# z products of a hybrid attention and DeltaNet layer, moved from the attention stage into the delta heads as filler

## Chip, cores and metric

One core of a Trainium2 chip. The metric is the device time of one launch in microseconds, median of three runs.

## The reference

One step of a one-layer encoder with 1024 prompt frames and 8 streams of 16 new frames, model width 1024, all float32:

```
x += 0.5 * SwiGLU_1(norm(x))
proj = norm(x) @ w_in      # q, k, v of 8 attention heads x 64; q, k, v, z of 4 delta heads x 128; beta, decay; 2 gates
yA = softmax attention over the frame's chunk of 64 and 8 chunks before it, with a bias by clipped distance
q, k, v = silu(causal conv of width 4 over proj)        # delta heads; q and k are l2-normalised
ob = gated delta rule (q, k, v, decay, beta), from a triangular solve per block and a scan over the blocks
ob = rmsnorm(ob) * silu(z)
x += (sigmoid(gA) * (yA @ w_branch_a) + sigmoid(gB) * (ob @ w_branch_b)) @ w_mix_out
x += CrossAttn(norm(x), 256 memory tokens)
x += 0.5 * SwiGLU_2(norm(x));  y = final_norm(x)
```

z of a delta head is thus 128 columns of `w_in`; it is first used when the head's output is scaled.

## The kernel before

Feature rows lie on the 128 partitions and all 1152 frames (1024 + 8 x 16) along the free dimension, cut in three thirds of 384. A weight matrix is cut into units of 128 output columns (128 x 1024). SP loads the units into a ring of three buffers (`load_units`, L72); GpSimd (POOL) splits each into an upper and a lower part (`split_units`, L107); TensorE multiplies. A **job** is one unit by one third: 24 products of 128x384 (8 chunks, each as upper by upper, upper by lower, lower by upper). Jobs write PSUM banks 0 and 1 in turn (`g % 2`); ACT evacuates a job's bank, and a job waits until the evacuation of the job that had its bank is counted. `slot` (L55) gives a unit its buffer of the ring.

A **Filler** (L222) cuts jobs into pieces, single products, and hands so many of them to each place of a plan, a list written out by hand: `products` (L238) issues the pieces of one place on TensorE, `finished` (L257) tells ACT which jobs end in a place, so that it evacuates them there.

**Attention** (`attention_phase`, L824): four pairs of heads. A pair has nine jobs of its own (v, q, k, three thirds each; `job` L975, `take` L1102 on ACT), then nine steps of scores, softmax and values (`pair`, L1020, L1128 and L1249), with the pieces of twelve filler jobs between them: the projections q, k, v and z of the delta head of the same number. ACT evacuates the rows of q, k and v into `stash`; DVE applies the convolution (`tap`, L1291) and ACT stores the result to DRAM (`store_row`, L1076). z is stored to DRAM as it is (L1072 to L1074). `turn_v` (L1004) transposes v on TensorE, `copy_v` (L1114) copies it back. The first pair takes its jobs third by third, and v is turned ahead of the last of them, with the first scores within it (`first_jobs`, L985). The three others run in a loop: on ACT, ten loads of bias rows (`load_bias`, L1091), the nine takes, and after the third of them the last conv row's store, the conv tail's store and the loads of the next head's conv state and weights (`next_conv`, L1086, `load_conv`, L1081); after the sixth, v's copies and the loads of the caches (`load_caches`, L1107).

**Delta** (`delta_phase`, L1521): four heads, one after the other, with twelve filler jobs each, the 16 units of the two branch gates; ACT evacuates them to `b_stash` and stores them (`evacuate_these`, L1785). A head on TensorE (`turn`, L1643): filler START; three groups of grams, decay rows and turns (L1656 to L1670), each with filler GROUP behind; filler BEFORE; the turns of Y (L1679); an inversion in 18 rounds over three groups of tiles (L1682 to L1696): a product P by the masked matrix (L1689), filler LEVEL, the turn of Y of two rounds ago (L1634), the correction of the round before (L1626); three W groups (L1703, L1705), with filler W; eight steps of the scan: a product by S (L1713), filler STEP, in steps 4 to 7 a sum of squares for the next head's keys (L1640), and three products (L1720 to L1724), of which DVE makes the next S (L2037); the samples, with two places SAMPLE; products by v8 (L1751); filler END; the three sums of squares for the output's norm (L1760), with filler LAST behind the first two. ACT loads z at round 12 (`load_z`, L1824), takes its silu ahead of step 0 (L1872), and at the head's end stores the states and, at the start of the next head, waits for those stores and loads the next states (L1831 to L1834). The output of head i - 1 is scaled by z in the rounds 6 to 11 of head i (`finish_output`, L1944). The plans count pieces per place (L1366); END takes what is left of 288:

```
PLAN, FIRST_PLAN = (28, 22, 20, 1, 8, 10, 10, 12), (0, 20, 14, 1, 8, 8, 8, 9)
#                   START, GROUP, BEFORE, LEVEL, W, STEP, SAMPLE, LAST
filler = Filler(3, 4, [0, 8, 20, 8, 22, 8, 24, 8] + [23, 8] + [30, 8] + [25, 8] * 3 + [6, 16])
```

Between the places of the attention's plan stand the turns of the probabilities, two per step. The phases and their units per turn are `turn_sizes` (L649); `weight_units` (host) lays out the units, and `nth_unit` (L760) reorders the first three of the attention.

Of the kernel before, what the change touches and what calls it, by code (L numbers as in the profile page):

```python
# [71 lines left out]
def load_units(sp, k, first, turns, turn, at_turn=None, then=None):  # L72
# [3 lines left out]
    def one(i, j):  # L76
        back, last = last_use(j, turn)
        if not (isinstance(i, int) and i < back):
            sp.wait_ge(k.unit_split.sem, k.unit_split.at(turn * i + (last + 1 - turn * back)))
        sp.dma_start(k.w_raw[slot(j, turn)][:, :], k.units[turn * i + (first + k.nth_unit(k.phase, j))])\  # L80
            .then_inc(k.raw_landed[slot(j, turn)].sem, 16)
# [7 lines left out]
    if turns > 1:  # L89
        with sp.Fori(1, turns) as i:  # L90
            if at_turn:
                at_turn(i)
            for j in range(turn):
                one(i, j)
    k.ahead = units_ahead(k)
    for j in range(k.ahead):
        users = sharing(j, turn) or [turn - 1]
        sp.wait_ge(k.unit_split.sem, k.unit_split.at(turn * (turns - 1) + users[-1] + 1))
        sp.dma_start(k.w_raw[j][:, :], k.units[first + turns * turn + k.nth_unit(k.phase + 1, j)]).then_inc(k.raw_landed[j].sem, 16)
# [122 lines left out]
class Filler:  # L222
# [4 lines left out]
    def __init__(self, main, units, plan, ahead=0):  # L227


        self.main, self.units, self.plan, self.ahead = main, units, plan, ahead  # L230
        self.count = 3 * units
# [6 lines left out]
    def products(self, k, pe, i, place, xh, xl):  # L238

        turn, per_turn = self.main + self.units, 3 * (self.main + self.units)  # L240
        first = sum(self.plan[:place])
        for m in range(first, first + self.plan[place]):
            g, r = 3 * self.main + m // self.PIECES, m % self.PIECES
            u, n, part, c = g // 3, g % 3, r // KD, r % KD
            if r == 0:
                if n == 0:
                    pe.wait_ge(k.unit_split.sem, k.unit_split.at(turn * i + (turn * self.ahead + u + 1)))

                pe.wait_ge(k.evacuated.sem, k.evacuated.at(per_turn * i + (per_turn * self.ahead + g + 1)))
            w = (k.w_lo if part == 2 else k.w_hi)[slot(u, turn)]  # L250
# [391 lines left out]
class Core:  # L642


    def __init__(self, nc, ctx):
# [3 lines left out]
        self.turn_sizes, self.phase, self.ahead, self.split_ahead = (2 * KD, 6, 7, 4, KD, KD, 2, KD, 6), 0, 0, False  # L649
# [110 lines left out]
    def nth_unit(self, phase, j):  # L760

        return (2, 0, 1)[j] if phase == 2 and j < 3 else j
# [61 lines left out]
def attention_phase(nc, k, norm, decay, head, xh, xl, x, x_to, work):  # L824
# [31 lines left out]
    filler = Filler(3, 4, [0, 8, 20, 8, 22, 8, 24, 8] + [23, 8] + [30, 8] + [25, 8] * 3 + [6, 16])  # L856

    DONE = 9 + filler.count
# [17 lines left out]
    def sync(sp):  # L876
# [7 lines left out]
        load_units(sp, k, k.next_unit, PAIRS, 7, then=store_x)  # L884

    def gpsimd(pool):
        split_units(pool, k, PAIRS, filler.jobs(), (7, 8) + filler.jobs()[2:], (0, 0, 0))

    def tensor(pe):
# [85 lines left out]
        def job(i, g, u, n, between=None):  # L975
            if n == 0:
                pe.wait_ge(k.unit_split.sem, k.unit_split.at(7 * i + (u + 1)))

            pe.wait_ge(k.evacuated.sem, k.evacuated.at(DONE * i + max(g + 1, 2)))
            tiles = [(k.w_hi[u][:, c * P:(c + 1) * P], k.w_lo[u][:, c * P:(c + 1) * P],  # L980
# [4 lines left out]
        def first_jobs():  # L985
            for n in range(3):
# [6 lines left out]
                for u in range(3):  # L993
                    if (n, u) == (2, 2):
                        turn_v(0)
                        job(0, 8, u, n, lambda: first_scores(0))
                        continue
# [22 lines left out]
        def pair(i):  # L1020
            for s in range(STEPS):
# [7 lines left out]
                filler.products(k, pe, i, 2 * s, xh, xl)  # L1029
# [3 lines left out]
                filler.products(k, pe, i, 2 * s + 1, xh, xl)  # L1033
                turn_probs(i, s, 1)
            filler.products(k, pe, i, 2 * STEPS, xh, xl)
            values(i, STEPS - 1)
            filler.products(k, pe, i, 2 * STEPS + 1, xh, xl)

        first_jobs()
        pair(0)  # L1040
        with pe.Fori(1, PAIRS) as i:
            for g in range(9):
# [3 lines left out]
                if g == 5:  # L1046
# [4 lines left out]
    def scalar(act):  # L1051
        def evacuate(i, g):
# [4 lines left out]
            if n == 0 and u == 1:  # L1057
                act.wait_ge(k.z_stored.sem, k.z_stored.at(16 * i + 16))
            elif n == 0:
                act.wait_ge(k.convolved.sem, k.convolved.at(3 * i + (0, 0, 1, 2)[u] + 1))  # L1060
            if u == 3:
                act.activation(row[:, CW - 1 + n * THIRD:CW - 1 + (n + 1) * THIRD], src[:, 0:THIRD], ACT.Copy)\
                    .then_inc(k.evacuated.sem, 1)
            elif n < 2:
# [7 lines left out]
            if n == 2 and u == 3:  # L1072
# [1839 lines left out]
```

## Time and profile before

| | |
|---|---|
| median of 3 runs | 3450.75 us (3444.57 to 3454.02) |
| profiled execution | 3447.24 us, span of its instructions 3445.5 us |
| TensorE products / weight loads busy | 3254.2 us (94%) / 3093.1 us (90%) |
| DVE / ACT / GpSimd busy | 37% / 20% / 28% |
| granted TensorE clock, mean | 0.983 |
| attention | about 980 to 1470 us: first pair to 1097.3, then 1222.1, 1346.6, 1469.9 |
| delta stage | 1470 to 2000 us: heads end (last sum of squares) at 1612.9, 1744.1, 1875.8, 2000.4 |

How to read it: PE is TensorE, PEld its weight loads, POOL GpSimd; ACTq is ACT's queue at work on an issue of a DMA. The ends of matmuls are modelled, so two rows overlap, and how long work takes is read from start to start. A granted clock of 1.00 is 2.4 GHz, 0.50 is 1.2 GHz. A row `x8` stands for eight instructions that follow each other; a float32 product of 128 columns counts as two.

### The profile page before, as it was taken

What the parts mean: (1) busy time and instruction counts of PE and PEld (TensorE: products, weight loads), DVE (VectorE), ACT (ScalarE), POOL (GpSimd) and SP (SyncE); (2) the same over time, 40 slices, a digit from 0 to 9 for tenths busy, and PEclk for the clock granted to TensorE, in tenths of its full rate; (3) what the DMA queues carried; (4) which work ended last, traced back from release to release, by engine and by line L of the source; (5) the groups of instructions that cost most, each with busy time, mean ns of one, the idle gap of its engine ahead of it and who ended that gap; (6) DMA issues with size and microseconds to landing.
All of it is one profiled execution on the core that took longest, in us unless ns stands there. A gap on an engine that the chain in (4) does not pass through costs nothing. (4 is left out here: it accounts for less than half of the span.)

```text
span 3445.5 us, 50361 instructions
## 1 busy us (share of the span) xinstructions
PE 3254.2 (94%) x19977; PEld 3093.1 (90%) x19977; DVE 1286.4 (37%) x2289; ACT 681.7 (20%) x1318; POOL 947.6 (28%) x436
## 2 busy tenths in 40 slices
PE   6999999999989999989998979999799999999998
PEld 5999999999878889888887879988598999999997
DVE  3232333333435635643442454331225323233324
ACT  5100000000123323344433332133311000000001
POOL 3433333333312223111001023221123333333331
PEclk9999999999999999999999999999899999999999
DMA  5311111111232232212112144024401111111111
GB/s 189 136 37 49 43 43 43 42 37 37 86 115 78 101 127 92 108 48 84 70 48 86 44 158 158 25 99 150 148 31 43 43 47 39 42 43 43 37 49 55
DMA packets 96544, 254.05 MB, mean 74 GB/s; under 512 B 11552, under 2 KB 52640, under 8 KB 93728
## 3 DMA queue, kind: packets, MB, share of 16 engines
q1 hardware_dynamic: 45568, 146.95, 13.0%
q10 hardware_dynamic: 50848, 105.25, 8.5%
q8 instruction: 97, 1.59, 0.2%
q14 instruction: 31, 0.25, 0.0%
HBM read 199.83 MB, written 52.33 MB: 73 GB/s over the span
## 5 line engine op out<-in xcount | busy, mean ns | idle before, releaser
L124 POOL TENSOR_TENSOR w_hi<-w_raw,zero 128x1024 fp32r<-128x1024 f32 x201 | 384.5, 1913 | 2221.2 <-PE psum L157 1324.4
L157 PE MATMUL psum<-x_hi,w_hi 128*128 128x384 f32 x3024 | 597.1, 337 | 44.6 <-DVE x_lo L2254 32.5
L157 PE MATMUL psum<-x_lo,w_hi 128*128 128x384 f32 x3024 | 595.7, 337 | 0.0
L157 PE MATMUL psum<-x_hi,w_lo 128*128 128x384 f32 x3024 | 590.0, 334 | 0.0
L157 PEld LDWEIGHTS psum<-x_hi,w_hi 128*128 128x128 f32 x3024 | 532.5, 189 | 54.5 <-issue 46.6
L157 PEld LDWEIGHTS psum<-x_lo,w_hi 128*128 128x128 f32 x3024 | 534.7, 189 | 2.1 <-issue 0.2
L157 PEld LDWEIGHTS psum<-x_hi,w_lo 128*128 128x128 f32 x3024 | 531.3, 188 | 0.0
L127 POOL TENSOR_TENSOR w_lo<-w_raw,w_hi 128x1024 fp32r<-128x1024 f32 x201 | 494.4, 2460 | 15.8
L407 DVE TENSOR_TENSOR f_hid<-psum,f_gate 128x384 f32<-128x384 f32 x132 | 73.6, 557 | 857.5 <-PE psum L157 857.5
L357 ACT ACTIVATE f_gate<-psum 128x384 f32<-128x384 f32 x132 | 64.8, 493 | 1478.2 <-PE psum L157 1474.5
L157 PE MATMUL psum<-f_h_hi,w_hi 128*128 128x384 f32 x1056 | 269.5, 336 | 0.0
L157 PE MATMUL psum<-f_h_lo,w_hi 128*128 128x384 f32 x1056 | 267.9, 334 | 0.0
L157 PE MATMUL psum<-f_h_hi,w_lo 128*128 128x384 f32 x1056 | 267.9, 334 | 0.0
L251 PE MATMUL psum<-x_hi,w_hi 128*128 128x384 f32 x912 | 203.4, 351 | 0.6 <-POOL w_lo L127 0.5
L251 PE MATMUL psum<-x_lo,w_hi 128*128 128x384 f32 x912 | 199.3, 347 | 0.0
L251 PE MATMUL psum<-x_hi,w_lo 128*128 128x384 f32 x912 | 198.1, 346 | 0.0
L157 PEld LDWEIGHTS psum<-f_h_hi,w_hi 128*128 128x128 f32 x1056 | 190.4, 188 | 3.6 <-issue 1.2
L157 PEld LDWEIGHTS psum<-f_h_lo,w_hi 128*128 128x128 f32 x1056 | 190.7, 188 | 0.0
L157 PEld LDWEIGHTS psum<-f_h_hi,w_lo 128*128 128x128 f32 x1056 | 190.6, 188 | 0.0
L422 DVE SCALAR_TENSOR_TENSOR x_late<-psum,x_late 128x384 f32<-128x384 f32 x264 | 145.1, 556 | 109.9 <-PE psum L157 109.9
L422 DVE SCALAR_TENSOR_TENSOR x_early<-psum,x_early 128x384 f32<-128x384 f32 x264 | 145.0, 556 | 107.2 <-PE psum L157 107.0
L251 PEld LDWEIGHTS psum<-x_hi,w_hi 128*128 128x128 f32 x912 | 159.8, 190 | 6.0 <-issue 2.7
(283 smaller groups left out, 3274.0 us busy)
## 6 DMA issues: line engine op xcount, KB each, us to landing
w_raw<-units SPq DMA_DIRECT2D x224, 512.0 KB, 3.6
gate_dram<-b_stash ACTq DMA_DIRECT2D x48, 192.0 KB, 1.9
e_gate<-gate_dram ACTq DMA_DIRECT2D x48, 192.0 KB, 2.5
a_kc<-k_cache ACTq DMA_DIRECT2D x4, 2048.0 KB, 8.9
a_vc<-v_cache ACTq DMA_DIRECT2D x4, 2048.0 KB, 14.7
x_sk<-mem_k ACTq DMA_DIRECT2D x8, 1024.0 KB, 9.0
proj_dram<-a_cv ACTq DMA_DIRECT2D x12, 576.0 KB, 2.7
b_pad<-proj_dram SPq DMA_DIRECT2D x12, 576.0 KB, 5.3
```

Of the source, the lines that this page charges most:

```text
L124: pool.tensor_tensor(k.w_hi[s][:, :], k.w_raw[s][:, :], k.zero[:, 0:1].to_broadcast([P, D]), ALU.add)\
L127: pool.tensor_tensor(k.w_lo[s][:, :], k.w_raw[s][:, :], k.w_hi[s][:, :].bitcast(F32), ALU.subtract).then_inc(k.unit_split.sem, 1)
L157: mm = pe.matmul(out, wl if part == 2 else wh, (xl if part == 1 else xh)[:, n0:n1], start=(part == 0 and i == 0), stop=(part == 2 and i == ...
L251: mm = pe.matmul(k.ps[g % 2][:, 0:THIRD], w[:, c * P:(c + 1) * P], (xl if part == 1 else xh)[:, c, n * THIRD:(n + 1) * THIRD], start=(r == 0),
L357: act.activation(gate[:, n, :], k.ps[g % NPS][:, 0:THIRD], ACT.Silu).then_inc(k.gate_ready.sem, 1)
L407: dve.tensor_tensor(hid[:, j % 2, :], up, gate[:, n, :], ALU.mult).then_inc(k.hid_made.sem, 1)
L422: dve.scalar_tensor_tensor(out=xs, in0=k.ps[g % NPS][:, 0:THIRD], scalar=0.5, in1=xs, op0=ALU.mult, op1=ALU.add).then_inc(k.x_added.sem, 1)
```

## The change

z of delta head 0 stays filler of the attention, in the last pair; z of heads 1 to 3 becomes the third of five filler units in its own head, and ACT copies it into its tile in SBUF without a way through DRAM. In the attention, v of the next pair takes z's place as filler; pairs 1 to 3 begin with q. The first pair's turn of v and first scores come behind its last job, and its plan has 14 pieces in the first place. On ACT, the last conv row's store and the conv loads come ahead of the first take of pairs 1 to 3; silu(z) moves into step 3. The delta plans get new places: AFTER (behind the turns of Y), a second one per round (behind the correction) and a second one per step (behind its last product). The filler's first job of a turn now waits for two evacuations at once (`max(g + 1, 2)`), as a head of 15 jobs ends in the bank in which the next one starts.

```
-PLAN, FIRST_PLAN = (28, 22, 20, 1, 8, 10, 10, 12), (0, 20, 14, 1, 8, 8, 8, 9)
+PLAN, FIRST_PLAN = (30, 22, 14, 10, (1, 2), 8, 10, 1, 6, 9), (0, 18, 14, 6, (0, 1), 8, 7, 0, 5, 8)
...
+    def head_plan(own, units, start, group, before, after, level, w, step, behind, sample, last):
+        p = own + [start] + [group] * 3 + [before, after] + list(level) * LV + [w] * 3 + [step, behind] * 8 + \
+            [sample] * 2 + [0] + [last] * 2
+        p[-3] = 3 * units * Filler.PIECES - sum(p)
...
+    later_heads = Filler(0, 5, head_plan([], 5, *PLAN), shift=-1)
+    first_head = Filler(0, 4, head_plan([36] + [6] * KEYS, 4, *FIRST_PLAN))
...
+            fill(pe, i, AFTER)
             pe.wait_ge(k.x_started.sem, k.x_started.at(3 * i + 3))
...
-                fill(pe, i, LEVEL + r)
+                fill(pe, i, LEVEL + 2 * r)
                 if 2 <= r < LV - 1:
                     turn_level(pe, i, r - 2)
                 if r >= 1:
                     correct(pe, i, r - 1)
+                fill(pe, i, LEVEL + 2 * r + 1)
...
-                fill(pe, i, STEP + t)
+                fill(pe, i, STEP + 2 * t)
...
                     .then_inc(k.o_done.sem, 1)
+                fill(pe, i, STEP + 2 * t + 1)
...
             for g in products:
-                act.wait_ge(k.dense_done.sem, k.dense_done.at(12 * i + (g + 1)))
+                act.wait_ge(k.dense_done.sem, k.dense_done.at(jobs_to(i) + (g + 1)))
+                if later and g // 3 == ZED:
+                    act.wait_ge(k.o_scaled.sem, k.o_scaled.at(3 * i))
+                    act.activation(z[:, third(g % 3)], k.ps[g % ND][:, 0:THIRD], ACT.Copy).then_inc(k.evacuated.sem, 1)
+                    continue
...
-            act.wait_ge(k.z_landed.sem, k.z_landed.at(16 * i + 16))
-            act.activation(z[:, :], z[:, :], ACT.Silu).then_inc(k.silued.sem, 1)
...
                 if t == 3:
+                    if isinstance(i, int) and i == 0:
+                        act.wait_ge(k.z_landed.sem, k.z_landed.at(16))
+                    else:
+                        act.wait_ge(k.evacuated.sem, k.evacuated.at(15 * i + (6 + ND)))
+                    act.activation(z[:, :], z[:, :], ACT.Silu).then_inc(k.silued.sem, 1)
...
 # Filler.products: the wait of a job
-                pe.wait_ge(k.evacuated.sem, k.evacuated.at(per_turn * i + (per_turn * self.ahead + g + 1)))
+                pe.wait_ge(k.evacuated.sem, k.evacuated.at(per_turn * i + (per_turn * self.ahead + 3 * self.shift + max(g + 1, 2))))
...
 # attention
+    first_pair = Filler(3, 4, period=6, slots=FIRST_SLOTS, plan=[14, 8, 18, 8, 20, 8, 22, 8] + [23, 8] + [30, 8] + [23, 8] * 3 + [6, 14])
+    later_pairs = Filler(3, 4, period=6, slots=LATER_SLOTS, plan=[0, 8, 20, 8, 22, 8, 24, 8] + [23, 8] + [30, 8] + [25, 8] * 3 + [6, 16])
...
         first_jobs()
+        turn_v(0)
+        first_scores(0)
         pair(0)
         with pe.Fori(1, PAIRS) as i:
-            for g in range(9):
+            for g in range(3, 9):
                 if g == 8:
                     first_scores(i)
                 job(i, g, g // 3, g % 3)
-                if g == 5:
+                if g == 3:
                     turn_v(i)
...
+        copy_v(0)
         pair(0)
         with act.Fori(1, PAIRS) as i:
             load_bias(i)
-            for g in range(9):
-                if g == 0:
+            next_conv(i - 1)
+            load_conv(i)
+            for g in range(3, 9):
+                if g == 3:
                     act.wait_ge(k.kv_stored.sem, k.kv_stored.at(32 * i + 32))
...
-                if g == 2:
-                    next_conv(i - 1)
-                    load_conv(i)
-                if g == 5:
+                if g == 3:
                     copy_v(i)
                     load_caches(i)
```

Units: 7 in the first turn of the attention (with v of pair 1), 6 in each of the next three (the sixth is v of the next pair, in the last turn z of head 0), 4 in delta head 0 and 5 in each later one. `host_unit` takes them from the host's unchanged order, and SP's loops run their last turn unrolled. In all, the attention has 75 jobs for 84, the delta heads 57 for 48.

## Rows read from the trace of the kernel before

Columns of the windows: stretch and length in us; busy us and count (x) of PE, PEld, DVE, ACT, POOL; granted clock; DMA share; GB/s. Columns of a timeline: start, us, engine, line, operation, out<-in, count, and in brackets the idle time before it and who ended it.

**Rows 1.** Windows: attention pair 1; 4 us of head 0; delta heads 1, 2, 3.

```profile
1097.30:1222.10 124.80, 122.17 (x872) 110.74 (x872) 62.23 (x113) 39.95 (x95) 30.91 (x15) 1.00 0.29 105
1482.00:1486.00 4.00, 4.00 (x11) 3.09 (x11) 1.15 (x2) 1.62 (x4) 0.00 (x0) 0.50 0.05 17
1612.90:1744.10 131.20, 118.90 (x791) 108.87 (x790) 51.74 (x111) 49.23 (x99) 17.03 (x8) 1.00 0.19 66
1744.10:1875.80 131.70, 118.91 (x791) 108.86 (x791) 51.72 (x111) 49.22 (x99) 17.02 (x8) 1.00 0.18 65
1875.80:2000.40 124.60, 114.53 (x781) 106.87 (x780) 50.31 (x108) 37.06 (x78) 16.96 (x8) 1.00 0.16 55
```

**Rows 2.** Waits of TensorE in the attention: us in total, times, longest.

```profile
PE psum L939 <- DVE a_sc L1288: 10.4, 9, 7.3
PE psum L157 <- ACT a_stash L1062: 2.6, 3, 1.2
```

**Rows 3.** Waits of TensorE in the delta heads, the same columns.

```profile
PE psum L1689 <- DVE b_MT L2000: 6.3, 4, 2.2
...
PE psum L1656 <- DVE b_vb L1980: 5.2, 3, 2.1
```

**Rows 4.** Timeline of PE, start of pair 1: start, duration, instructions.

```profile
1098.83 1.55 PE L157 MATMUL psum<-x_lo,w_hi 128*128 128x384 f32 x8
1100.21 1.55 PE L157 MATMUL psum<-x_hi,w_lo 128*128 128x384 f32 x8
```

**Rows 5.** Timeline of ACT and its queue (ACTq), start of pair 1.

```profile
1096.78 0.49 ACT L1062 ACTIVATE a_stash<-psum 128x384 f32<-128x384 f32 x1 [2.71 <-PE psum L251]
...
1098.45 0.62 ACTq L1100 DMA_DIRECT2D a_bias<-bias_dram  x1
...
1104.46 0.49 ACT L1104 ACTIVATE a_v<-psum 128x384 f32<-128x384 f32 x1 [7.19 <-issue]
...
1110.38 0.40 ACTq L1079 DMA_DIRECT2D proj_dram<-a_cv  x1
...
1112.33 0.36 ACTq L1084 DMA_DIRECT2D a_cw<-conv_w  x1
```

**Rows 6.** Timeline of PE, first pair.

```profile
999.58 0.80 PE L894 MATMUL psum<-a_k,a_q 64*128 64x128 f32 x4 [2.38 <-ACT a_vns L1119]
...
1011.89 0.48 PE L939 MATMUL psum<-ident,a_sc 128*128 128x128 f32 x1 [7.33 <-DVE a_sc L1288]
```

**Rows 7.** Timelines of ACT's queue and of DVE, first pair.

```profile
1001.25 1.86 ACTq L1100 DMA_DIRECT2D a_bias_s<-bias_dram  x4
...
1007.51 0.11 DVE L1258 MEMSET a_bias<- 64x64 f32 x1 [8.86 <-DMA a_bias_s<-bias_dram]
```

**Rows 8.** Timeline of ACT, end of head 1 and start of head 2.

```profile
1745.99 0.48 ACT L1791 ACTIVATE b_stash<-psum 128x384 f32<-128x384 f32 x1
...
1753.54 0.49 ACT L1838 ACTIVATE b_eg<-psum 128x384 f32<-128x384 f32 x1 [0.65 <-ACT b_stash L1791]
```

**Rows 9.** Timeline of PE, one round of the inversion of head 1.

```profile
1656.13 0.94 PE L1689 MATMUL psum<-b_X,b_MT 128*128 128x128 f32 x6
...
1658.16 0.94 PE L1689 MATMUL psum<-b_X,b_MT 128*128 128x128 f32 x6
```

**Rows 10.** Timeline of ACT, the same round.

```profile
1657.11 0.49 ACT L1853 ACTIVATE b_P<-psum 128x384 f32<-128x384 f32 x1 [1.02 <-PE psum L1689]
1657.62 0.49 ACT L1857 ACTIVATE b_X<-psum 128x384 f32<-128x384 f32 x1
```

**Rows 11.** Timeline of PE, end of a step of head 1.

```profile
1699.11 0.39 PE L1724 MATMUL psum<-b_intra,b_vw 128*128 128x128 f32 x2
1699.71 0.49 PE L1713 MATMUL psum<-b_S,b_wT 128*128 128x128 f32 x2 [0.22 <-DVE b_S L2037]
```

**Rows 12.** Timeline of PE, END of head 1.

```profile
1734.86 1.96 PE L251 MATMUL psum<-x_hi,w_lo 128*128 128x384 f32 x8
1738.54 0.91 PE L1760 MATMUL psum<-b_sq,ones 128*128 128x384 f32 x2 [1.73 <-ACT b_sq L1805]
```

More of the change, by code:

```diff
@@ L69, in last_use, with load_units @@
     return (0, same[at - 1]) if at else (1, same[-1])
-def load_units(sp, k, first, turns, turn, at_turn=None, then=None):
+def load_units(sp, k, first, turns, turn, at_turn=None, then=None, apart=0):
     def one(i, j):
@@ L89, in load_units @@
     if turns > 1:
-        with sp.Fori(1, turns) as i:
+        with sp.Fori(1, turns - apart) as i:
             if at_turn:
@@ L94, in load_units @@
                 one(i, j)
+    for i in range(turns - apart, turns):
+        if at_turn:
+            at_turn(i)
+        for j in range(turn):
+            one(i, j)
     k.ahead = units_ahead(k)
@@ L238, in products @@
     def products(self, k, pe, i, place, xh, xl):
-        turn, per_turn = self.main + self.units, 3 * (self.main + self.units)
+        turn, per_turn = self.period, 3 * self.period
+        slots = self.slots or [slot(u, turn) for u in range(turn)]
         first = sum(self.plan[:place])
@@ L1176, in pair @@
                     store_row(i, STORE[s])
-                for g in filler.finished(2 * s):
+                for g in filler_of(i).finished(2 * s):
                     evacuate(i, g)
@@ L1561, in delta_phase, with jobs_to @@
     OUT_FROM = 6
[L1565 to L1566 removed]
+    START, GROUP, BEFORE, AFTER, LEVEL = 0, 1, 4, 5, 6
+    W = LEVEL + 2 * LV
+    STEP, SAMPLE, END, LAST = W + 3, W + 19, W + 21, W + 22
+    ZED = 2
     OWN = 1 + KEYS
[L1569 to L1576 removed]
+    def head_plan(own, units, start, group, before, after, level, w, step, behind, sample, last):
+        p = own + [start] + [group] * 3 + [before, after] + list(level) * LV + [w] * 3 + [step, behind] * 8 + \
+            [sample] * 2 + [0] + [last] * 2
+        p[-3] = 3 * units * Filler.PIECES - sum(p)
+        return p
+    later_heads = Filler(0, 5, head_plan([], 5, *PLAN), shift=-1)
+    first_head = Filler(0, 4, head_plan([36] + [6] * KEYS, 4, *FIRST_PLAN))
+    def jobs_to(i):
+        return 0 if isinstance(i, int) and i == 0 else 15 * i - 3
     def fill(pe, i, place):
```

155 lines of the change are left out of this document (88 added, 67 removed).

## The prediction

> **What bounds the kernel now.** I read the windows by stage first. In an attention pair after the first TensorE is busy 122.2 of 124.8 us; in a delta head 118.9 of 131.2 us, and its weight loads 108.9 us [rows 1]. So the attention is TensorE from end to end, and the delta heads have some room. Then the waits of TensorE in the attention: 10.4 us for the softmax, 7.3 us of it once, and 2.6 us at the three starts of a pair [rows 2]; and those in the delta stage, where DVE and ACT let it wait in many places [rows 3]. Last the timelines, because the waits don't show everything: ends of matmuls are modelled, and a short wait disappears in the tail of the one before it. Only distances from start to start tell what a piece of filler costs.
>
> The unit of everything below: eight 128x384 products start 1.39 us apart from the next eight [rows 4], so a piece is 0.1735 us and a job (24 pieces) 4.16 us, wherever TensorE has nothing to wait for. The change moves nine jobs, 216 pieces (z of heads 1 to 3), from the attention, where they cost all of their time, into three delta heads, 72 pieces each, where they cost what the waits there don't swallow.
>
> **The attention.** (a) Pairs 1 to 3 lose their three leading v jobs: 9 x 4.16 = -37.5 us. The filler stays 12 jobs per pair, with the next v in z's place.
>
> (b) The starts of pairs 1 to 3. Today job 0 waits for the last evacuation (2.6 us in three) [rows 2], since both have bank 0. The new first job (g = 3) has the other bank, and that wait goes: -2.6. What is late next is ACT's queue. ACT ends the last evacuation at 1097.3, then issues the ten bias loads from 1098.45 on, and takes the first third at 1104.46 [rows 5]. Now the store of the last conv row, its tail and the two conv loads stand ahead of that take; they run from 1110.38 to 1112.7 today, 2.3 us [rows 5]. The z store (0.4 us) is gone. So the first take comes at about 1106.4. TensorE, started at 1096.7, does a job, the 16 turns of v (0.11 us each, estimated from the 0.67 us that six such products take) and a second job, until 1106.8, and its third job needs that first take, done at 1107.0: 0.2 us. In the other two pairs the bias issues last longer, and the same sum gives 0.8 and 0.3. Together -2.6 + 1.3 = -1.3 us. Bounds: -2.6, if nothing is late, and +3, if each issue is as slow as the slowest row. The caches are issued after one q job instead of after the third; 4 MB have over 40 us to land, so nothing.
>
> (c) The first pair. Today TensorE stands 2.4 us for the copy of turned v, does the scores and the rest of job 8, and stands 7.3 us until the first probabilities, at 1011.9 [rows 6]. What they wait for is DVE, which waited until 1007.5 for the bias rows [rows 7], whose last issue ended at 1003.1, behind the copies of v. The change puts both copies behind job 8 and so behind the bias issues: these end some 4 us earlier, and the probabilities come at about 1007.9, -4.0 us. By then 38 pieces are done instead of 24: the 14 moved there lay in the wait, -2.4 us. They are missing later, in steps that have small waits for the softmax already; I put +1.5 back. Sum -4.9 us; bounds -7 and -1 (if the bias rows land no earlier, since other transfers share that time).
>
> **A later delta head, from one last sum of squares to the next.** START has 30 pieces for 28, and each head now begins with a bank that the last job of the head before holds. That wait is new: ACT makes two root steps and then the evacuation that today runs from 1745.99 to 1746.5 [rows 8], so TensorE stands some 2.1 us. Behind it stand START and the group's products; who waits for those? Group 1, and it waits today for DVE (5.2 us in three heads) [rows 3], which got its first row from ACT at 1753.54, after the store and the load of the states [rows 8]. That chain doesn't move, so the new wait takes the place of the old one: +0.5, 0 and +0.8 us in the three heads. Before the inversion, 6 pieces less and 10 more behind the turns, where TensorE stands 1.4 to 2.2 us for the first mask (6.3 us in four heads) [rows 3]: the filler there covers it, and what is ahead shortens: -0.7.
>
> The inversion: 18 rounds. A round takes 2.02 us from start to start [rows 9], while its products, free of waits, need 1.84 (15 square ones of 0.11 us and a piece). ACT sets the 2.02: copy of P, copy of X, 0.49 us each [rows 10], one of them behind the product and one ahead of the next. With one piece ahead of the correction and two behind, a round needs 1.84 + 0.35 = 2.19 of TensorE, and ACT no longer sets it. 36 pieces more (+6.25) swallow 0.17 x 18 = 3.1, and part of the stop at the output's store, where ACT no longer loads z: 0.2. So +2.95. In between nothing changes; z is copied by ACT without a store, once per third.
>
> The eight steps: today a step's tail waits for S on DVE, 0.60 us from the last product to the next, where 0.22 is work [rows 11]. One piece goes in there and 10 stay: 8 pieces at nothing. The cover is this wait alone: if the piece delays the next product, it is +1.4. silu(z) now stands in ACT's queue at step 3, ahead of the table load and of the first key square, where a step of 3.1 us has room for it.
>
> The sample part loses 8 pieces, of which 4 lay in a wait for ACT: -0.7 (head 3, without key sums, -1.4). END gets 44 pieces for 8. Today it ends with a wait (3.68 us for 1.39 us of work) [rows 12]: the job's evacuation, its store and the square come 2.0 us after the job. Now the last job in END stops 6 pieces ahead of its end, so 1.0 of this is covered: +6.25 - 1.0 = +5.2. The last two fillings lose 6 pieces: -1.0.
>
> Sum: head 1 6.4, head 2 5.8, head 3 5.9, together +18.1 of the 37.5 moved. Head 0 only reorders its 288 pieces: groups and steps shorter (-1.4), inversion -0.5, sample -0.5, last -0.35, END with 16 more pieces +3.1: +0.3. Bounds for the four heads: +12 (the rounds keep 2.02 and swallow more of their waits by the two new places) and +31 (only the END and mask waits are swallowed).
>
> POOL and SP: 5 units per head, one per 15 to 20 us; nothing waits. SP waits for W of a head before it loads the next pad and the units behind it, as today.
>
> **A page against the rows.** TensorE's matmul row is busy 91% in a head, its weight loads 83% [rows 1]. The Trainium skill (Perfetto Trace Analysis, Identifying the Most-Contended Engine) holds the first for a bad measure and wants the second. The rounds agree: no idle time in the matmul row, yet 0.18 us free. Read alone, the loads' share would leave 22 us in each head, more than the 12.5 moved there, and the sum would be that of rival A. I don't go by it, since END and half of each round are work on a full engine.
>
> **Sum.** -37.5 - 1.3 - 4.9 + 18.1 + 0.3 = -25.3 us. The profiled execution took 3447.24 us (span 3445.5 and 1.7 around it); it stands 3.5 below the median of the three runs, inside their spread. Forecast **3422 us**; with the bounds of (c) and of the rounds 3414 to 3430.
>
> **Rivals.**
> A, all is hidden: the heads take up all 37.5 us. For: a head has 12.3 us in which no matmul runs and 12.5 are added. Against: END is filler alone for 36 pieces. Time 3447.2 - 37.5 - 6.2 + 0.3 = 3404. Chance 0.07.
> B, nothing is hidden: the waits sit on chains that the filler pushes along, piece by piece (P to its copy to the correction), so moved work costs the same as before: 3447.2 - 6.2 + 0.3 = 3441, no change. For: in head 0 the distance of the rounds is set by ACT, and filler ahead of a product delays it. Against: two pieces of three stand behind the correction. Also what would show if the moved z did nothing of what the change says. Chance 0.10.
> C, a part is given back by queues: ACT late at all three starts (3 each) and at the new head starts: some +11, 3433. Chance 0.06.
> D, slower, by the clock: behind a wait TensorE has run at 1.2 GHz (granted 0.50 in 1482 to 1486, after a wait for the first key square) [rows 1]. If the new 2.1 us waits at three head starts let it fall to that level and it stayed there through an inversion, 18 rounds would cost 1.8 us more each, 32 us per head. From about 20 rounds at this level the gain is gone and 10 us more; with two heads 3486. Against: a later head with waits of 1.7 and 2.1 us had 1.00 throughout [rows 1]. [...] Chance 0.03.
>
> **How the numbers follow.** Forecast 0.74. What a measurement of this kernel can tell from no change is 0.3%, 10.3 us, so faster ends at 3436.9. Faster: forecast, A and C, 0.87. Same: B, 0.10. Slower: D, 0.03. The range leaves out most of A, B and D: 3410 to 3437.
>
> **What would show it.** Pairs 1 to 3 at about 112 us, starts with under 1 us of wait; first probabilities near 1008. Rounds of 2.19 us; a wait of some 2 us at each head start and less than 0.5 us in front of group 1; a step still 3.12 us with 11 pieces; END near 8.9 us from v8 to the first square; later heads at 137, 137 and 130 us. Rounds of 2.37 us, or steps of 3.3, would prove B; a pair of 115 us C; granted clocks of 0.5 in an inversion D.

## The result, and the profile after

The changed kernel takes 3433.23 us, median of 7 runs (3428.33 to 3437.7); the kernel before, run beside it, 3452.44 us (7 runs, 3444.57 to 3456.68). The ratio is 0.9947, 95% interval [0.9936, 0.9957]: faster by 18 us, give or take 4. Forecast were 3422 us and a gain of 25.3.

The profiled execution took 3437.7 us (span 3435.9), the highest of its seven, while the profiled one of before was below its median. The two spans are therefore only 9.6 us apart. So I read both kernels in sections between fixed matmuls of TensorE, and profiled both a second time. "Start" is the first matmul on the b_w8h columns ahead of the attention (941.23 in the first profile of before), "attention" runs from there to the block sums, "heads" from the block sums to the last square sum of head 3.

| us | before | before, again | after | after, again | forecast |
|---|---|---|---|---|---|
| span | 3445.5 | 3449.6 | 3435.9 | 3433.5 | |
| start | 941.2 | 945.0 | 945.4 | 942.8 | no change |
| attention | 528.7 | 529.0 | 482.0 | 484.4 | -43.7 |
| head 0, from the block sums | 142.9 | 142.9 | 146.6 | 144.8 | +0.3 |
| head 1 | 131.2 | 131.3 | 142.6 | 142.0 | +6.4 |
| head 2 | 131.7 | 131.8 | 140.1 | 139.2 | +5.8 |
| head 3 | 124.5 | 124.0 | 134.8 | 133.6 | +5.9 |
| behind the heads | 1445.1 | 1445.7 | 1444.4 | 1446.8 | no change |

The attention gave 3 us more than forecast (1 in the second profile), the four heads cost 15 more (11). Attention and heads together gain 13.1 and 14.9 us in the two pairs of profiles, less than the 18 of the ratio: both profiled executions of the changed kernel lie above their medians. The windows show the heads: the DMA share is little changed, DVE is busy 2 to 5 us longer per head, and the granted clock, 1.00 in all three before [rows 1], is now 0.96, 0.99 and 0.97; in 8 us of head 3 it is 0.63. Windows of after: pair 1 (from turn of v to turn of v), heads 1, 2, 3, and those 8 us; columns as in [rows 1].

```profile
1093.40:1207.00 113.60, 110.02 (x801) 98.07 (x800) 64.34 (x113) 38.41 (x92) 30.73 (x15) 1.00 0.32 112
1574.10:1716.60 142.50, 133.18 (x863) 121.84 (x862) 57.03 (x111) 50.32 (x102) 22.66 (x10) 0.96 0.17 60
1716.60:1856.80 140.20, 130.94 (x865) 120.14 (x864) 56.51 (x111) 50.33 (x102) 23.07 (x10) 0.99 0.17 61
1856.80:1991.50 134.70, 127.44 (x851) 120.30 (x850) 52.21 (x107) 38.28 (x81) 23.83 (x10) 0.97 0.13 47
...
1872.00:1880.00 8.00, 5.21 (x24) 5.24 (x25) 3.51 (x9) 1.34 (x3) 0.00 (x0) 0.63 0.00 0
```

Waits of TensorE in heads 1 to 3 of after (us in total, times, longest):

```profile
PE psum L1683 <- ACT b_sq L1857: 5.6, 6, 1.7
PE psum L258 <- ACT b_stash L1843: 4.9, 3, 1.7
PE psum L1699 <- DVE b_vb L2037: 4.1, 2, 2.9
PE psum L1677 <- DVE b_Y L2068: 2.6, 3, 1.9
...
PE psum L1733 <- DVE b_MT L2057: 1.6, 3, 0.7
```

L1699 <- b_vb and L1733 <- b_MT answer to [rows 3]. The second row is the forecast wait at each head start. The wait for b_Y and the one for a mask inside the inversion are new, and so is the size of the first row: 3.9 us in six in before.

The first pair: TensorE's timeline of after, answering to [rows 6]. The two waits are 1.22 and 1.48 us for 2.38 and 7.33.

```profile
1005.43 0.49 PE L924 MATMUL psum<-a_k,a_q 64*128 64x128 f32 x4 [1.22 <-ACT a_vns L1146]
1005.85 1.66 PE L258 MATMUL psum<-x_hi,w_hi 128*128 128x384 f32 x8
...
1010.04 0.33 PE L969 MATMUL psum<-ident,a_sc 128*128 128x128 f32 x1 [1.48 <-DVE a_sc L1316]
```

Two rounds of the inversion of head 1, answering to [rows 9]: 2.20 us, as forecast.

```profile
1622.59 0.83 PE L1733 MATMUL psum<-b_X,b_MT 128*128 128x128 f32 x6
...
1624.79 0.83 PE L1733 MATMUL psum<-b_X,b_MT 128*128 128x128 f32 x6
```

### The profile page after: what moved, and what is told of

Same layout as the page of the kernel before. It is cut to its first block and busy times, and to the rows that moved or that the text cites. A ratio compares the mean times of both kernels' runs of the same rounds, so it can differ in the third digit from the quotient of the medians.

```text
span 3435.9 us, 50179 instructions
## 1 busy us (share of the span) xinstructions
PE 3254.4 (95%) x19977; PEld 3087.9 (90%) x19977; DVE 1311.4 (38%) x2289; ACT 678.8 (20%) x1318; POOL 954.7 (28%) x436
## 5 line engine op out<-in xcount | busy, mean ns | idle before, releaser
L162 PE MATMUL psum<-x_lo,w_hi 128*128 128x384 f32 x2952 | 581.0, 336 | 0.0
L162 PEld LDWEIGHTS psum<-x_lo,w_hi 128*128 128x128 f32 x2952 | 521.7, 189 | 1.9
L162 PEld LDWEIGHTS psum<-x_hi,w_lo 128*128 128x128 f32 x2952 | 518.8, 188 | 0.0
L258 PE MATMUL psum<-x_lo,w_hi 128*128 128x384 f32 x984 | 224.2, 351 | 0.0
L258 PEld LDWEIGHTS psum<-x_hi,w_hi 128*128 128x128 f32 x984 | 170.0, 189 | 12.2 <-ACT b_stash L1843 4.4
```

The costliest lines, as they stand in the source:

```text
L162: mm = pe.matmul(out, wl if part == 2 else wh, (xl if part == 1 else xh)[:, n0:n1], start=(part == 0 and i == 0), stop=(part == 2 and i == ...
L258: mm = pe.matmul(k.ps[g % 2][:, 0:THIRD], w[:, c * P:(c + 1) * P], (xl if part == 1 else xh)[:, c, n * THIRD:(n + 1) * THIRD], start=(r == 0),
```

## The experiments

**Theory.** The rounds, the steps and the END of head 3 cost what was forecast; the rest of the loss is (1) POOL's split of a weight unit, which now falls into the inversion and holds DVE up, (2) TensorE's clock, which falls behind waits of 1.7 to 2.9 us, (3) ACT's queue at the start of a head. **Rivals:** nothing is swallowed in the rounds; the new wait at a head's start is itself the loss; what is dear comes and goes with the single execution.

All runs but one were timed several times beside the kernel before. The sections are those of each run's profile.

| | median us | ratio to before, 95% | attention | heads |
|---|---|---|---|---|
| after (twice) | 3433.2, 3432.8 | 0.9947 [0.9936, 0.9957], 0.9944 [0.9932, 0.9956] | 482.0, 484.4 | 564.0, 559.5 |
| first pair back | 3444.8 | 0.9986 [0.9977, 0.9994] | 494.2 | 560.0 |
| rounds with one piece | 3434.2 | 0.9953 [0.9941, 0.9965] | 481.8 | 563.0 |
| head 0's places back | 3428.5 | 0.9937 [0.9923, 0.9950] | 482.3 | 555.6 |
| splits held back | 3428.3 | 0.9939 [0.9925, 0.9953] | 482.6 | 554.2 |
| evacuation ahead | 3420.6 | 0.9912 [0.9898, 0.9926] | 481.7 | 553.8 |
| stores ahead too | 3420.1 | 0.9913 [0.9900, 0.9925] | 485.4 | 550.7 |
| sample pieces | 3428.3 | 0.9935 [0.9922, 0.9947] | 482.2 | 556.0 |
| loops written out | 3424.3 | 0.9926 [0.9913, 0.9939] | 478.9 | 553.3 |
| together | 3408.8 | 0.9879 [0.9864, 0.9893] | 481.9 | 538.8 |
| together, written out | 3410.9 | 0.9876 [0.9862, 0.9890] | 479.4 | 537.0 |

An interval of 0.0013 is 4.5 us, so a difference of a few us between two runs is read from the sections and not from the medians.

### The kernel before, again

> The kernel before itself, for a second profile. In five profiles of changed kernels TensorE waits 2.3 us near 124 us for the gate of the first feed-forward part, whose ACT row stands behind a copy of the bias rows on DVE, and their attention begins 4 to 5.5 us later than in the profile of before. If that wait comes and goes by itself (the theory), it can be in this profile too, and the attention begins 3 to 5 us later than 941.2. If the change brings it (rival), this profile begins its attention at 941 again.

Its one execution took 3451.34 us, the start is at 945.0, and the wait is there. TensorE, then DVE, of this second profile of before:

```profile
125.84 2.66 PE L157 MATMUL psum<-x_hi,w_hi 128*128 128x384 f32 x8 [2.32 <-ACT f_gate L357]
```

```profile
120.40 3.07 DVE L789 COPY bias_rows<-bias_rows 128x4088 f32<-128x4088 f32 x1 [33.41 <-DMA bias_rows<-table]
```

So 4 us of what the two first spans hide is not the change's. The other sections of before repeat within 0.6 us, which makes sections the better scale; those of the changed kernel repeat less well, within 1.8 us per head and 2.4 in the attention.

### The first pair back

```diff
-    first_pair = Filler(3, 4, period=6, slots=FIRST_SLOTS, plan=[14, 8, 18, 8, 20, 8, 22, 8] + [23, 8] + [30, 8] + [23, 8] * 3 + [6, 14])
+    first_pair = Filler(3, 4, period=6, slots=FIRST_SLOTS, plan=[0, 8, 20, 8, 22, 8, 24, 8] + [23, 8] + [30, 8] + [25, 8] * 3 + [6, 16])
...
                 for u in range(3):
+                    if (n, u) == (2, 2):
+                        turn_v(0)
+                        job(0, 8, u, n, lambda: first_scores(0))
+                        continue
...
+                copy_v(0)
                 load_bias(0)
-        copy_v(0)
```

> The changed kernel with the first attention pair as before (its filler plan, and the turns of v and their copies back inside job 8). Theory: the first pair brought 4.9 us, so this takes 4.9 us more than the changed kernel (3433 to 3438), and the first probabilities come near 1012 again. Rival: the probabilities were not what the pair waited for, the gain of the attention came from the missing jobs alone: no more than 1 us.

The attention takes 494.2 us for 482.0: the first pair brought 12.2 us, not 4.9, and the median is 11 us up. Most runs with the new first pair have 481.7 to 482.6; the second profile of after has 484.4, with its clock down for some 3 us in the first pair, and against it the gain is 9.8. TensorE in the first pair of this run:

```profile
1005.05 0.80 PE L924 MATMUL psum<-a_k,a_q 64*128 64x128 f32 x4 [2.38 <-ACT a_vns L1148]
1005.78 2.85 PE L162 MATMUL psum<-x_lo,w_hi 128*128 128x384 f32 x8
...
1017.36 0.48 PE L969 MATMUL psum<-ident,a_sc 128*128 128x128 f32 x1 [7.34 <-DVE a_sc L1318]
1017.49 2.91 PE L258 MATMUL psum<-x_hi,w_hi 128*128 128x384 f32 x8
```

The waits are 2.38 + 7.34 for 1.22 + 1.48: 7.0 us. Most of the rest is clock. Behind each wait eight products take 2.85 to 2.91 us, the level of 1.2 GHz, where they take 1.66 behind the first short wait of after; the granted clock of the whole first pair is 0.96 here and in before, and 1.00 in after. Some 8 us of work at half speed make 4 us, an estimate from the stretches of low clock in this trace.

### The rounds with one piece

```diff
-PLAN, FIRST_PLAN = (30, 22, 14, 10, (1, 2), 8, 10, 1, 6, 9), (0, 18, 14, 6, (0, 1), 8, 7, 0, 5, 8)
+PLAN, FIRST_PLAN = (30, 22, 14, 10, (1, 0), 20, 10, 1, 6, 9), (0, 18, 14, 6, (0, 1), 8, 7, 0, 5, 8)
```

> The changed kernel with one piece in a round of the inversion, as before, and the 36 pieces taken out put into the W part (20 for 8). Forecast's theory: rounds of 2.02 us for 2.19 (3.1 us less), 36 pieces at their full 6.25 us in the W part, so 3.1 us more per head and 9.4 in all: 3442. Rival (rounds swallow nothing more): no change, 3433. A third theory says that the split of a weight unit by POOL, which this plan moves from the inversion to the W part, slows DVE where it falls: then head 1 gains back the 2.2 us of waits for the mask and Y, and the sum is 5 to 8 us more, 3438 to 3441.

The time is that of the first rival, no change (3434.2 us), but not for its reason. The inversions take 35.12, 35.12 and 35.73 us for 42.60, 39.80 and 39.68, 16 us less, and the W parts give 5.6 each back, 17 us in all. Rounds are 2.02 us again (TensorE of this run):

```profile
1623.11 0.94 PE L1733 MATMUL psum<-b_X,b_MT 128*128 128x128 f32 x6
1625.13 0.94 PE L1733 MATMUL psum<-b_X,b_MT 128*128 128x128 f32 x6
```

The two pieces per round are half free, as forecast, so by them alone this plan would lose 9 us. It gains as much elsewhere, as the third theory has it: no split falls into its inversion, and the inversion is 0.6 to 1.2 us shorter than in before, where a round waits for the output's store.

### Head 0's places back

```diff
-PLAN, FIRST_PLAN = (30, 22, 14, 10, (1, 2), 8, 10, 1, 6, 9), (0, 18, 14, 6, (0, 1), 8, 7, 0, 5, 8)
+PLAN, FIRST_PLAN = (30, 22, 14, 10, (1, 2), 8, 10, 1, 6, 9), (0, 20, 14, 0, (1, 0), 8, 8, 0, 8, 9)
```

> The changed kernel with head 0's places of filler as before. Forecast's theory: head 0's new places cost 0.3 us, so this is the same within the measurement, 3433. Rival, from the profile after (head 0 at 121.2 us for 116.7): the new places cost 4.5 us, 16 pieces more in the END part at full price and a wait of 1.8 us in front of group 1, so this takes 4.5 us less, 3429, END back at 5.3 us less.

Head 0 is back at 142.9 us, from 146.6 and 144.8; END from the v8 products to the first square at 2.17 us from 7.50, and the wait of 1.8 us in front of group 1 is gone. This speaks for the rival. But two later runs limit it: with the loops written out and the new places head 0 takes 142.9 us too, and with the old places in "together" it takes 144.5, with 1.4 us of that wait. So the wait comes and goes with something other than the places, and what the places cost by themselves is between 0 and 2.5 us, an estimate from head 0's time less that wait in the runs of the table.

### The splits held back

```diff
             used = first if isinstance(i, int) else jobs
+            if late and j in late:
+                late[j](pool, i)
...
-        split_units(pool, k, HB - 1, (3, 6, 9, 12, 15), None, (-9, 0, -3))
+        split_units(pool, k, HB - 1, (3, 6, 9, 12, 15), None, (-9, 0, -3), {
+            4: lambda e, i: e.wait_ge(k.wu_done.sem, k.wu_done.at(3 * i + 6)),
+            0: lambda e, i: e.wait_ge(k.kv_done.sem, k.kv_done.at(9 * i + 10))})
```

> The changed kernel, with two of the five splits of a later head held back on POOL: the one in the inversion until the W products are done, the one in the sample part until the END part. Theory (POOL slows DVE's work in SBUF while it splits a unit, and TensorE waits for DVE there): mask and Y of head 1 back at 0.55 us, the 2.2 us of waits gone, key scales in the sample part back below 1.2 us, in all 3 to 8 us less than the changed kernel, 3425 to 3430. Rival: POOL is off the path, DVE's slow instructions have another cause: no change, 3433.

This is the cleanest result. In after, POOL, DVE and TensorE in head 1:

```profile
1625.03 1.89 POOL L129 TENSOR_TENSOR w_hi<-w_raw,zero 128x1024 fp32r<-128x1024 f32 x1 [24.58 <-PE psum L258]
1627.00 2.55 POOL L132 TENSOR_TENSOR w_lo<-w_raw,w_hi 128x1024 fp32r<-128x1024 f32 x1
```

```profile
1622.91 0.55 DVE L2057 TENSOR_TENSOR b_MT<-b_NT,b_consts 128x384 f32<-128x384 f32 x1
1624.64 0.55 DVE L2068 TENSOR_TENSOR b_Y<-b_Y,psum 128x384 f32<-128x384 f32 x1 [1.18 <-PE psum L1669]
1625.11 2.23 DVE L2057 TENSOR_TENSOR b_MT<-b_NT,b_consts 128x384 f32<-128x384 f32 x1
1627.26 2.70 DVE L2005 SCALAR_TENSOR_TENSOR b_oT<-b_oT,b_gn,b_ro 128x384 f32<-128x384 f32 x1
1629.89 0.54 DVE L2068 TENSOR_TENSOR b_Y<-b_Y,psum 128x384 f32<-128x384 f32 x1
```

```profile
1627.47 0.93 PE L1733 MATMUL psum<-b_X,b_MT 128*128 128x128 f32 x6 [0.33 <-DVE b_MT L2057]
...
1630.49 0.55 PE L1677 MATMUL psum<-ident,b_Y 128*128 128x128 f32 x3 [1.91 <-DVE b_Y L2068]
...
1632.00 1.48 PE L1733 MATMUL psum<-b_X,b_MT 128*128 128x128 f32 x6
```

A DVE instruction that reads two tensors of SBUF and begins while one of POOL's runs ends 0.4 us behind POOL's: 2.23 us for 0.55, then 2.70 for 0.61. Y's subtraction behind them is late, TensorE waits 1.91 us, and its clock falls. With the split held back the two instructions take (DVE of that run):

```profile
1624.25 0.55 DVE L2061 TENSOR_TENSOR b_MT<-b_NT,b_consts 128x384 f32<-128x384 f32 x1
1624.72 0.61 DVE L2009 SCALAR_TENSOR_TENSOR b_oT<-b_oT,b_gn,b_ro 128x384 f32<-128x384 f32 x1
```

Every full round of the three inversions is then 2.19 to 2.21 us, where after has one of 3.5 to 3.6 in heads 2 and 3 and two slow ones in head 1 (4.5 and 3.7; 4.9 and 3.3 in the second profile). The inversions: 38.3, 38.3 and 38.2 us for 42.6, 39.8 and 39.7. The held split falls at the end of W and costs 0.7 to 0.9 there, which is why W in before was 1.1 us longer than in after: before's split fell there (its copy b_wz took 1.29 us, for 0.22 in after). In all the split's new place saves 4.9 us; the time is 3 to 5 us down, which the two intervals don't tell from nothing. The sections gain more (554.2 for 564.0 and 559.5), because head 3 also starts 4 to 5 us sooner, which the edit doesn't touch: see the store below. The sample part gained nothing, though the key scales are back at 0.56 us: it waits for ACT.

The Trainium skill (Advanced Engine Details and Errata, GPSIMD Details) says that POOL shares a read and a write interface with DVE and conflicts with DVE instructions that have two SBUF inputs; Trainium Architecture — The Big Picture (What this means for kernel authors) calls it an exclusive lock. The trace agrees for the two inputs. A subtraction that takes one from PSUM keeps its 0.54 us within a split (after, head 2):

```profile
1771.35 2.56 POOL L132 TENSOR_TENSOR w_lo<-w_raw,w_hi 128x1024 fp32r<-128x1024 f32 x1
```

```profile
1771.61 0.54 DVE L2068 TENSOR_TENSOR b_Y<-b_Y,psum 128x384 f32<-128x384 f32 x1
```

The trace of before had it already. In its head 0 a split met DVE just ahead of the inversion, an instruction of 0.56 us took 2.13, and the longest wait of [rows 3], 2.2 us for the mask, came next:

```profile
1519.70 2.15 POOL L124 TENSOR_TENSOR w_hi<-w_raw,zero 128x1024 fp32r<-128x1024 f32 x1 [40.86 <-PE psum L251]
```

```profile
1520.14 2.13 DVE L1992 SCALAR_TENSOR_TENSOR b_Y<-b_MT,ident 128x384 f32<-128x384 f32 x1
```

### The evacuation ahead, and the stores ahead too

```diff
+                if g == 3:
+                    evacuate(i, LAST + 1)
                 if g >= 1:
                     root(ro[:, g - 1, :], first + g - 1, bank(2, g - 1), 1.0 / DHB)
-                if g >= 2:
-                    evacuate(i, LAST + g - 2)
+                if g == 2:
+                    evacuate(i, LAST)
```

> The changed kernel, with the evacuation of the last filler job of a head put ahead of the last root on ACT. Theory (group 1 waits for ACT's queue through DVE: the stores of the states, their load, the exponential): the wait at a head's start falls by 1.1 us, and group 1 comes no earlier, so no more than 1 us in all, 3433. Rival (the new wait at the head's start is itself the loss): 1.1 us less at three starts and the clock does not fall behind it, 3 to 5 us less, 3429.

The second run also moves the two stores:

```diff
                 if g == 3:
+                    act.wait_ge(k.s_final.sem, k.s_final.at(i + 1))
+                    act.dma_start(k.p_s_out[i], S[:, 0, :]).then_inc(k.s_out.sem, 16)
+                    act.dma_start(k.s_s_out[i], Sb[:]).then_inc(k.s_out.sem, 16)
                     evacuate(i, LAST + 1)
```

> As the run before, and the two stores of the states as well ahead of the last root and of that evacuation. Theory (ACT's queue with the states sets group 1): the stores start 2 us earlier, so does the exponential of group 0; the wait at the start falls by 1 us and the one in front of group 1 by 1 to 2 us, 2 to 3 us less per later head, 3425 to 3428. Rival (landing of the stores is what is late and is not sooner, since other transfers share it): the same as the run before within 1 us.

From the last square sum to group 0 heads 1 and 3 take 6.1 us for 7.7 and 7.8 with the evacuation alone, head 2 still 7.5. In front of group 1 head 1 gives 0.25 us back, head 2 nothing, and head 3 is 2.5 shorter on top (7.7 us from group 0 to group 1 for 10.3). The time is 11 us down, so my claim of 1 us at most is refuted. With the stores ahead too, all three take the bare 7.17 us to group 1. The loss of head 3 in after is the store's. ACT's queue there, then the same store in "first pair back", whose heads are those of after:

```profile
1860.28 2.12 ACTq L1964 DMA_DIRECT2D s_s_out<-b_Sb  x1
...
1869.24 0.49 ACT L1890 ACTIVATE b_eg<-psum 128x384 f32<-128x384 f32 x1 [0.43 <-ACT b_stash L1843]
```

```profile
1875.09 0.42 ACTq L1966 DMA_DIRECT2D s_s_out<-b_Sb  x1
```

That is 12.5 us from the last square sum to the exponential, for 8.7 in head 3 of before and 9.4 in head 2 [rows 8]; the store's issue takes 2.12 us and it lands after 6.5. Of the eight profiles that have the stores where after has them, five show 1.9 to 2.3 us for this issue in head 3, both of after among them; first pair back, splits held back and loops written out show 0.42, and head 3 takes 128.7 to 129.4 us in these for 131.9 to 135.2. Nothing in these three edits touches the store, so this loss comes and goes for a reason that I did not look for, and what head 3 gained in the run with the evacuation ahead can't be put down to the evacuation. By the ratios the two runs gain 11 us each on after. Their heads gain 6 and 9 on the second profile of after, 10 and 13 on the first; so the size of the gain is uncertain by some us, and the difference between the two runs isn't seen in their times.

### The sample pieces

```diff
-PLAN, FIRST_PLAN = (30, 22, 14, 10, (1, 2), 8, 10, 1, 6, 9), (0, 18, 14, 6, (0, 1), 8, 7, 0, 5, 8)
+PLAN, FIRST_PLAN = (30, 22, 14, 10, (1, 2), 8, 10, 1, 10, 9), (0, 18, 14, 6, (0, 1), 8, 7, 0, 5, 8)
```

> The changed kernel with 10 pieces in each of the two places of the sample part, as before, and 8 fewer in the END part. Forecast's theory: 4 of 8 pieces lie in the wait there, 0.7 us less per head but for head 3, where nothing changes: 1.4 us less. Theory from the profile after (TensorE stands 1.8 us for the key square in front of v8, and its clock falls behind it): 1.5 us more of clock in heads 1 and 2, 4 to 5 us less in all, 3429. Rival (the wait only moves along): no change.

The wait for the last key square falls from 1.74 to 1.04 us. In head 1 the clock now holds behind it, in head 2 it doesn't: the four v8 products take 1.98 and 3.23 us. Of after (head 1, then head 3, which has no key sums) and of this run (head 2), TensorE:

```profile
1697.90 1.65 PE L1683 MATMUL psum<-b_sq,ones 128*128 128x384 f32 x2 [1.74 <-ACT b_sq L1857]
1700.22 3.55 PE L1797 MATMUL psum<-b_v,b_kd 128*128 128x512 f32 x4 [0.67 <-ACT b_rr L1861]
...
1977.02 1.88 PE L1797 MATMUL psum<-b_v,b_kd 128*128 128x512 f32 x4
```

```profile
1831.94 0.91 PE L1683 MATMUL psum<-b_sq,ones 128*128 128x384 f32 x2 [1.04 <-ACT b_sq L1857]
1833.52 3.23 PE L1797 MATMUL psum<-b_v,b_kd 128*128 128x512 f32 x4 [0.67 <-ACT b_rr L1861]
```

The time fell by 3 to 4 us by the ratio, inside the interval. The mechanism is seen, and its price too (1.5 us or so where the clock falls), but not that fewer pieces there always bring it on: in the second profile of after, head 2 waits 1.74 us as well and its v8 products take 1.98 us.

### The loops written out

```diff
-        with pe.Fori(1, PAIRS) as i:
+        for i in range(1, PAIRS):
...
-        with pe.Fori(1, HB - 1) as i:
+        for i in range(1, HB - 1):
```

The three places that know the first pair by its index being a constant ask for 0 instead.

> The changed kernel with TensorE's loops over the pairs and over the heads written out, nothing else. Theory (the waits of 1.5 and 1.1 us at the starts of pairs 2 and 3, and 1.4 us at the start of head 2, are the jump back of TensorE's loop and no wait for a bank): pairs 2 and 3 start without a wait, 2.6 us less; head 2's start keeps its wait for the bank, which hides the jump, so 7.7 us there as now; in all 2 to 3 us less than the changed kernel. Rival (they are waits for the evacuation on ACT): no change.

The theory holds for the pairs. In the second profile of after, then in this run, TensorE at the start of pair 2:

```profile
1198.94 1.55 PE L258 MATMUL psum<-x_hi,w_lo 128*128 128x384 f32 x8
1202.20 1.67 PE L162 MATMUL psum<-x_hi,w_hi 128*128 128x384 f32 x8 [1.71 <-issue]
```

```profile
1192.95 1.55 PE L258 MATMUL psum<-x_hi,w_lo 128*128 128x384 f32 x8
1194.34 1.55 PE L162 MATMUL psum<-x_hi,w_hi 128*128 128x384 f32 x8
```

3.26 us from start to start against 1.39, and the same start was put down to ACT's a_v in the first profile (1.49 us). Head 2's start keeps its 7.8 us. The attention is 3 us shorter. The rest of the 6 us by the ratio lies in the heads: the waits in front of group 1 are gone in all four, which the edit was not expected to do and which I can't explain.

### Together, and together written out

```diff
-PLAN, FIRST_PLAN = (30, 22, 14, 10, (1, 2), 8, 10, 1, 6, 9), (0, 18, 14, 6, (0, 1), 8, 7, 0, 5, 8)
+PLAN, FIRST_PLAN = (30, 22, 14, 10, (1, 2), 8, 10, 1, (6, 16), 9), (0, 20, 14, 0, (1, 0), 8, 8, 0, (8, 8), 9)
```

and the edits of "splits held back" and "stores ahead too"; the last run adds that of "loops written out".

> Head 0's places as before, the two splits held back, stores and last evacuation ahead of the last root, and the sample part with 6 and 16 pieces and END with 34. By the runs so far: head 0 -4, splits -4, start of the heads -7, the wait of 1.0 us for the last key square covered and the slow clock behind it gone, -2 to -4: 15 to 19 us less than the changed kernel, 3414 to 3418. Rival (they overlap, each shortens the same wait or the same slow clock): no more than 12 less than it, 3421, as the run with the stores ahead alone.

> The run before with TensorE's two loops written out. Theory: 2.6 us less at pairs 2 and 3, and 1.2 us less at the start of head 2, whose 7.3 us come down to the 6.1 to 6.4 of heads 1 and 3, now that the evacuation is no longer what is late there: 3 to 4 us less. Rival (other causes at the starts): no change.

3408.8 us, ratio 0.9879 [0.9864, 0.9893], 23 us less than the changed kernel by the ratios. The heads gain 20.7 us on the second profile of after, a little more than the 15 to 19 expected of all, and the rival (they overlap, 12 at most) is refuted. But not every part is there: heads 1 to 3 bring 20.4 of it, and head 0, with its old places, takes 144.5 us. TensorE's windows of heads 1 to 3 in this run, at a clock of 1.00 throughout:

```profile
1566.40:1699.60 133.20, 128.71 (x864) 119.62 (x862) 52.01 (x111) 50.44 (x102) 21.33 (x10) 1.00 0.18 65
1699.60:1834.00 134.40, 128.80 (x864) 119.66 (x864) 52.17 (x111) 50.45 (x102) 21.34 (x10) 1.00 0.18 64
1834.00:1960.70 126.70, 123.81 (x852) 117.52 (x851) 50.03 (x107) 38.39 (x81) 23.23 (x10) 1.00 0.14 50
```

and its waits there:

```profile
PE psum L1762 <- DVE b_S L2086: 3.0, 3, 1.1
PE psum L1687 <- ACT b_sq L1861: 2.2, 4, 0.6
...
PE psum L260 <- ACT b_stash L1847: 1.2, 2, 0.9
```

The three later heads cost 6.8 us more than in before, for the 37.5 moved out of the attention. With the loops written out the profile has 4 us less (attention 2.5, heads 1.8; head 2's start 6.40 us for 7.08), as expected; the times don't tell the two apart.

## Why the prediction was right, and where it was wrong

The range and the sign held, and the gain in the sum, 25.3 us, was 6 to 7 us too good; another 5 us of the 11 between 3422 and 3433.2 are its base, a profiled execution that lies 5 us under the median of before measured beside. That the forecast came so near was partly luck, because errors of both signs met. By the sections, forecast / measured:

- **(a) and (b), pairs 1 to 3**: -38.8 / -34.6 (529 to 494.2, with the first pair as before). Nine jobs went at their price. The step that failed is "that wait goes: -2.6": I read the 2.6 us at three starts [rows 2] as a wait for a bank. At pairs 2 and 3 it stood over a jump back of TensorE's loop, which takes 1.3 to 1.9 us by itself, shown by the loops written out; the waits there are 1.49 and 1.10 us in after, 2.6 again. Of ACT's late takes, +1.3, only the 0.2 us of pair 1 showed. Another 0.6 to 0.8 us per pair behind its start lies in small waits for the softmax; I didn't test them.
- **(c), the first pair**: -4.9 / -12.2 (-9.8 by the second profile). The mechanism held (probabilities at 1010.0 in an execution that starts 4.2 later, so 1005.8 for the 1007.9 forecast); the term was mis-sized twice. No +1.5 came back, since the small waits of the steps were 0.7 us in before and 0.04 in after, and the clock was left out: [rows 6] were there, and the products behind them ran at half speed.
- **Before the inversion**: -0.7 / -0.8. **Rounds**: 2.19 / 2.19 to 2.21. **Inversion**: +2.95 / +2.5, +2.5 and +1.3 with the split held back, but +6.8, +4.0 and +2.7 as the change stands. The step that failed is "POOL and SP: 5 units per head ... nothing waits": true of them, and not the question. What they hold up is DVE. I counted the units and not where their splits fall, and I took the longest wait of [rows 3] for DVE's own, though a split lay over it.
- **W**: 0 / -1.1, the other side of the same: a split left it.
- **Steps**: the piece behind each was at nothing, 29.27 / 29.27 us.
- **Sample part**: -0.7, -0.7, -1.4 / +0.2, -0.6, -1.4. **END**: +5.2 / +6.8, +6.6, +5.1. Both are right in head 3 and, in the second profile, in END of head 2 (+5.2), and 0.8 to 1.6 us off where TensorE waited 1.74 + 0.67 us and the clock fell behind it. The failed step is a missing term: taking cover from a wait can cost more than the cover. The sign "END near 8.9 us from v8" was a slip by itself: 3.68 + 5.2 counts from the last filler row of [rows 12], and from v8 the forecast makes 5.1 + 5.2 = 10.3. And the terms of head 1 add up to 6.25 us, not 6.4. **LAST**: -1.0 / -1.05.
- **Head start with group 1**: +0.5, 0, +0.8 / +0.5, +1.2, +3.8, and another 2.9 us to group 2 in head 3 (0.63 clock behind a wait of 2.92; 1.6 us in the second profile). "That chain doesn't move" failed: ACT's chain came 1.2 and 3.8 us later in heads 2 and 3, by its DMA issues. With the evacuation ahead the wait at the start turned out to be a loss of its own, 1.4 us in head 1.
- **Head 0**: +0.3 / +3.6 and +1.9. Its END cost 5.3 us for 16 pieces, 3.1 forecast, and group 1 waited 1.8 us for DVE. Putting the old places back returned both, but the wait was back in "together" with the old places, so its cause stays open.

Of the rivals, C (queues) came true at one start in three, and D in small: no inversion ran at 1.2 GHz throughout, but stretches of 3 to 7 us behind waits did, for 1.5 us or so at a place. What I had against D, waits of 1.7 and 2.1 us with a clock of 1.00 [rows 1], was no rule. A was refuted by the rounds and END, B by the rounds and the steps.

## What to carry to other kernels

When filler is moved, list what its progress triggers: each finished unit lets another engine start, and in the new place that work may take the port of the engine which the stage waits for. Such work can be held back by one wait: here it then cost 0.7 to 0.9 us at the end of W for 1.5 to 4.3 in the inversion, so look for a place where nobody is in need of the port. Price a wait that is taken away or left without cover together with the slow products behind it, and before a wait is booked as a gain ask what else stands at the same place, a loop's jump for one.

## What the runs showed of the hardware that I had not expected

- POOL's tensor_tensor on 128x1024 holds a DVE instruction with two SBUF inputs that begins behind it until 0.4 us past its own end: 0.55 us became 2.23, 0.61 became 2.70. A copy of 128x128 within SBUF was held too, 1.29 us for 0.22; instructions with an input in PSUM were not.
- A jump back of TensorE's loop costs 1.3 to 1.9 us between eight products and the next eight, which otherwise start 1.39 us apart, and the profile puts it down to ACT in one execution and to "issue" in another. The Trainium skill (Advanced Engine Details and Errata, Control Flow Timing) gives branches at 51 and 108 ns; the measurement decides. Why it is so much more was not tried.
- After waits of 1.0 to 2.9 us TensorE was at 1.2 GHz in some executions and at 2.4 in others, at the same place of a head (v8 products 1.98 and 3.23 us in heads 1 and 2 of one run, behind the same waits of 1.04 and 0.67 us).
- The issue of one 512 KB store on ACT's queue took 0.42 us or 2.12 us at the same place, and its landing 2.8 to 4.4 or 6.5. It was the short one in three runs of eight, two of which have TensorE's loop as after has it. Left open.
